# A 31-tap depthwise convolution: 28 taps on TensorE instead of 32, three on VectorE, and two more phases brought over by ScalarE

## Time and profile before

| | us |
|---|---|
| median of 3 runs | 1105.55 (1104.82 to 1106.0) |
| the profiled execution, its time | 1104.8 |
| the profiled execution, its span | 1102.9 |
| TensorE busy | 1089.6, 99% of the span |
| VectorE busy | 668.8, 61% |
| GpSimd busy | 502.6, 46% |
| ScalarE busy | 465.4, 42% |

### The profile page before, as it was taken

The page is one execution under the profiler, slowest core; times in us unless marked ns, Lnnn a source line. Parts: engine busy times, 40 slices in busy tenths (PEclk is TensorE's granted clock), DMA queues, the critical chain, the costliest instruction groups (busy, mean ns, idle before and its releaser), DMA issues.

```text
span 1102.9 us, 16220 instructions
## 1 busy us (share of the span) xinstructions
PE 1089.6 (99%) x5922; PEld 879.0 (80%) x5922; DVE 668.8 (61%) x958; ACT 465.4 (42%) x808; POOL 502.6 (46%) x375
## 2 busy tenths in 40 slices
PE   9999999999999999999999999999999999999997
PEld 7786877788788888888888888877778778888786
DVE  6875986416666666666641222548754757986863
ACT  6436321354744333333333334345464543243663
POOL 5445341122455444444444445433347686632441
PEclk9999999999999999999999999999999999999999
DMA  9953532241223323232323325322115222212222
GB/s 246 136 85 56 67 70 39 84 108 39 78 90 102 114 76 114 76 114 76 114 74 98 105 78 152 115 77 77 39 52 140 54 80 78 77 40 78 77 77 77
DMA packets 101721, 97.28 MB, mean 88 GB/s; under 512 B 4896, under 2 KB 95776, under 8 KB 101280
## 3 DMA queue, kind: packets, MB, share of 16 engines
q1 hardware_dynamic: 101232, 95.71, 31.8%
q10 hardware_dynamic: 432, 0.79, 0.2%
HBM read 94.38 MB, written 2.10 MB: 87 GB/s over the span
## 4 chain that ended last, share of the span: by engine, by line
PE 91%; DVE 4%; ACT 2%; issue 1%; POOL 1%; DMA 1%; POOLq 0%; DVEq 0%; SPq 0%; ACTq 0%
PE ps L1914 26%; PE ps L1916 25%; PE ps L1915 25%; PE ps L2457 4%; PE ps L2118 1%; DVE x_a L1237 1%; DVE conv L1758 1%; PE ps L2392 1%; ACT x_a L674 1%; PE ps L2403 1%; PE ps L2304 1%; PE ps L2286 1%; DVE tt L1349 1%; POOL w_lo L536 1%; PE ps L2380 1%
## 5 line engine op out<-in xcount | busy, mean ns | idle before, releaser
L536 POOL TENSOR_TENSOR w_lo<-raw,w_hi 128x512 fp32r<-128x512 f32 (+1 forms) x330 | 447.9, 1368 | 568.1 <-ACT w_hi L657 557.5
L657 ACT ACTIVATE w_hi<-raw 128x512 fp32r<-128x512 f32 (+1 forms) x330 | 201.1, 620 | 254.1 <-PE ps L1916 237.2
L1914 PE MATMUL ps<-x_a,w_hi 128*128 128x512 f32 x624 | 251.8, 403 | 4.3 <-POOL w_lo L536 2.0
L1916 PE MATMUL ps<-x_a,w_lo 128*128 128x512 f32 x624 | 243.3, 390 | 0.0
L1915 PE MATMUL ps<-x_a,w_hi 128*128 128x512 f32 x624 | 243.3, 390 | 0.0
L1914 PE MATMUL ps<-x_b,w_hi 128*128 128x512 f32 x416 | 162.5, 391 | 0.1
L1915 PE MATMUL ps<-x_b,w_hi 128*128 128x512 f32 x416 | 161.9, 389 | 0.0
L1916 PE MATMUL ps<-x_b,w_lo 128*128 128x512 f32 x416 | 161.8, 389 | 0.0
L1914 PEld LDWEIGHTS ps<-x_a,w_hi 128*128 128x128 f32 x624 | 117.2, 188 | 38.9 <-issue 11.1
L1916 PEld LDWEIGHTS ps<-x_a,w_lo 128*128 128x128 f32 x624 | 117.1, 188 | 24.9
L1915 PEld LDWEIGHTS ps<-x_a,w_hi 128*128 128x128 f32 x624 | 117.3, 188 | 24.6 <-issue 2.2
(11 more groups left out here) (351 smaller groups left out, 1532.2 us busy)
## 6 DMA issues: line engine op xcount, KB each, us to landing
raw<-in_w_up SPq DMA_DIRECT2D x44, 512.0 KB, 4.4
raw<-in_w_in SPq DMA_DIRECT2D x31, 512.0 KB, 7.7
raw<-in_c_w_in SPq DMA_DIRECT2D x24, 512.0 KB, 4.7
raw<-in_a_w_in SPq DMA_DIRECT2D x18, 512.0 KB, 4.6
raw<-in_w_down SPq DMA_DIRECT2D x16, 512.0 KB, 4.4
raw<-in_w_out SPq DMA_DIRECT2D x8, 512.0 KB, 4.0
raw<-in_c_w_out SPq DMA_DIRECT2D x8, 512.0 KB, 4.1
raw<-in_w_down SPq DMA_DIRECT2D x8, 384.0 KB, 3.4
```

The lines of the kernel that those rows point to most:

```text
L536: nc.gpsimd.tensor_tensor(ring_half(WL, n), raw_half(n), f32(ring_half(WH, n)), SUB) \
L657: nc.scalar.activation(ring_half(WH, n), raw_half(n), ACT.Copy).then_inc(w_hi, 1)
L1914: mm(out, w_hi_, x_hi_, start=first, stop=False)
L1916: return mm(out, w_lo_, x_hi_, start=False, stop=last)
```

## The change

The zero tap is gone, and with it a whole step: TensorE does 7 steps of 4 phases, for taps 3 to 30 (`DIRECT` = 3). Taps 0 to 2 are added by VectorE from the unsplit `GLU`, over whole tiles of 128 partitions, in three dependent instructions (`add_direct`). ScalarE, besides phase 3, copies phases 2 and 1 into a new tile `PH`, in eight pieces of 32 partitions (`later_phases`); VectorE adds phase 0 out of PSUM in four pieces, and phases 2 and 1 from `PH` in two instructions over 128 partitions (`add_phases`). ScalarE's and VectorE's work on tile k moves from the end of iteration n = 2k + 4 into iteration n = 2k + 5: on VectorE `add_direct` comes before `evict(n)`, `add_phases` after it and before `glu`; on ScalarE `later_phases` comes after the first weight split. The eviction of the rough mean moves to the start of n = 9, the square of tile 7 on ScalarE to n = 20, of tile 6 to n = 18. The sum of tile 6's square goes behind the last `add_centered`.

```diff
-TAP_STEPS = 8
+TAP_STEPS = 7
+DIRECT = CK - TAP_PHASES * TAP_STEPS
-SQUARES_AT = {11: (0, 1), 13: (2, 3), 15: (4,), 17: (5,), 19: (6, 7)}
+SQUARES_AT = {11: (0, 1), 13: (2, 3), 15: (4,), 17: (5,), 18: (6,)}
+        PH = at("conv_phases", [P, 2, S], F32, AR + 45056)
...
-                                            EYE32[:, :].unsqueeze(1).broadcast_to([P, 32, 32]),
+                                            EYE32[:, :].unsqueeze(1).broadcast_to([P, CK - DIRECT, 32]),
...
-            def last_phase(k):
+            def later_phases(k):
                 act.wait_ge(cv_filled, k + 1)
                 for r in range(4):
                     nc.scalar.activation(CV[32 * r:32 * r + 32, k, :], PS[96:128, 4 + r, :], ACT.Copy) \
                         .then_inc(cv_copied, 1)
+                if k > 0:
+                    act.wait_ge(tile_whole, k)
+                for r in range(4):
+                    for q in (2, 1):
+                        nc.scalar.activation(PH[32 * r:32 * r + 32, q - 1, :], PS[32 * q:32 * q + 32, 4 + r, :],
+                                             ACT.Copy).then_inc(cv_copied, 1)
...
                 if n >= 3:
                     split_hi(2 * u + 3)
+                if n - 1 in CONV_AFTER:
+                    later_phases(CONV_AFTER[n - 1])
...
+                if n == 20:
+                    ln_square(7)
...
-                if n in CONV_AFTER:
-                    last_phase(CONV_AFTER[n])
...
                 if k >= 2:
                     dve.wait_ge(g_hi, k - 1)
                     dve.wait_ge(g_lo, k - 1)
+                    dve.wait_ge(direct_added, k - 1)
...
+            def add_direct(k):
+                dve.wait_ge(cv_copied, 12 * k + 4)
+                for i in range(DIRECT):
+                    by = CK - 1 - i
+                    y = CV[:, k, by:S]
+                    ins = v.scalar_tensor_tensor(out=y, in0=GLU[:, k % 2, 0:S - by], scalar=DCW[:, i, k:k + 1], in1=y,
+                                                 op0=MUL, op1=ADD)
+                    if i < DIRECT - 1:
+                        step(ins)
+                    else:
+                        ins.then_inc(direct_added, 1)
...
             def add_phases(k):
-                for q in (2, 1, 0):
-                    late_by = TAP_PHASES - 1 - q
-                    for r in range(4):
-                        if q == 2:
-                            dve.wait_ge(cv_copied, 4 * k + r + 1)
-                        else:
-                            dve.wait_ge(dchain, steps[0] - 3)
-                        y = CV[32 * r:32 * r + 32, k, late_by:S]
-                        ins = v.tensor_tensor(y, PS[32 * q:32 * q + 32, 4 + r, 0:S - late_by], y, ADD)
...
+                late_by = TAP_PHASES - 1
+                dve.wait_ge(direct_added, k + 1)
+                for r in range(4):
+                    dve.wait_ge(cv_copied, 12 * k + 4 + 2 * r + 2)
+                    y = CV[32 * r:32 * r + 32, k, late_by:S]
+                    v.tensor_tensor(y, PS[0:32, 4 + r, 0:S - late_by], y, ADD).then_inc(cv_ready, 1)
+                dve.wait_ge(cv_ready, 4 * k + 4)
+                for q in (2, 1):
                     late_by = TAP_PHASES - 1 - q
+                    y = CV[:, k, late_by:S]
+                    ins = v.tensor_tensor(y, PH[:, q - 1, 0:S - late_by], y, ADD)
+                    if q == 2:
+                        step(ins)
+                    else:
+                        ins.then_inc(tile_whole, 1)
...
             for n in range(24):
+                if n == SHIFT_AFTER + 1:
+                    dve.wait_ge(shift_filled, 1)
+                    v.tensor_scalar(MEAN, PS[:, (M7 + SHIFT_AFTER + 1) % 4, :], 1.0 / (2 * P), None, MUL) \
+                        .then_inc(bank_free, 1)
+                    dve.wait_ge(bank_free, M7 + SHIFT_AFTER + 2)
+                if n - 1 in CONV_AFTER:
+                    k = CONV_AFTER[n - 1]
+                    add_direct(k)
                 evict(n)
+                if n - 1 in CONV_AFTER:
+                    add_phases(k)
                 if n < 16 and n % 2 == 1:
                     glu(n // 2)
-                if n in CONV_AFTER:
-                    k = CONV_AFTER[n]
-                    add_phases(k)
+                if n - 1 in CONV_AFTER:
...
-                        else:
+                        elif k < KT - 1:
                             add_ln_square(k - 1)
                         add_centered(k)
                         if k == KT - 1:
+                            add_ln_square(k - 1)
                             add_ln_square(k)
...
                 if k >= 1:
-                    pe.wait_ge(cv_ready, k)
+                    pe.wait_ge(cv_ready, 4 * k)
```

More of the change, by code:

```diff
@@ L250, in build @@
         GL = at("glu_lo", [P, 2, GPW], F32R, A3 + 8416)
-        DCWH = at("tap_hi", [P, 32, KT], F32R, A3 + 12736)
-        DCWL = at("tap_lo", [P, 32, KT], F32R, A3 + 13760)
+        DCWH = at("tap_hi", [P, CK - DIRECT, KT], F32R, A3 + 12736)
+        DCWL = at("tap_lo", [P, CK - DIRECT, KT], F32R, A3 + 13760)
         EYE32 = at("eye32", [P, 32], F32, A3 + 14784)
@@ L333, in build @@
         g_hi, g_lo = sem("glu_hi_ready"), sem("glu_lo_ready")
-        cv_filled, cv_copied, cv_ready = sem("conv_filled"), sem("conv_phase_copied"), sem("conv_ready")
+        cv_filled, cv_copied, cv_ready = sem("conv_filled"), sem("conv_phases_copied"), sem("conv_ready")
+        direct_added, tile_whole = sem("direct_taps_added"), sem("conv_tile_whole")
         shift_sum, shift_filled = sem("shift_sum_ready"), sem("shift_filled")
@@ L582, in tap_parts_made @@
                 gp.wait_ge(tap_rounded, 1)
-                nc.gpsimd.tensor_tensor(DCWL[:, 1:32, :], DCW[:, :, :], f32(DCWH[:, 1:32, :]), SUB) \
+                nc.gpsimd.tensor_tensor(DCWL[:, :, :], DCW[:, DIRECT:CK, :], f32(DCWH[:, :, :]), SUB) \
                     .then_inc(tap_parts, 1)
-                gp.wait_ge(tap_parts, 9)
+                gp.wait_ge(tap_parts, 7)
             def tap_weights(k, parts=(0, 1)):
@@ L1070, in _ @@
                 if k == 1:
-                    nc.scalar.activation(DCWH[:, 1:32, :], DCW[:, :, :], ACT.Copy).then_inc(tap_rounded, 1)
+                    nc.scalar.activation(DCWH[:, :, :], DCW[:, DIRECT:CK, :], ACT.Copy).then_inc(tap_rounded, 1)
                 if k >= 1:
@@ L1096, in gated @@
                 act.wait_ge(glu_ready, k + 1)
-                act.wait_ge(tap_parts, 9)
+                act.wait_ge(tap_parts, 7)
                 if k >= 2:
@@ L1740, in glu @@
                 dve.wait_ge(g_hi, k + 1)
-                dve.wait_ge(tap_parts, 9)
+                dve.wait_ge(tap_parts, 7)
                 if k >= 2:
@@ L1765, in center @@
             def center(k):
-                dve.wait_ge(dchain, steps[0])
-                dve.wait_ge(cv_ready, k + 1)
+                dve.wait_ge(tile_whole, k + 1)
                 v.scalar_tensor_tensor(out=CV[:, k, :], in0=CV[:, k, :], scalar=vec("dw_b", k), in1=MEAN,
@@ L1819, in _ @@
             for n in range(24):
+                if n == SHIFT_AFTER + 1:
[6 more added lines that the diff above has]
+                    add_direct(k)
                 evict(n)
+                if n - 1 in CONV_AFTER:
+                    add_phases(k)
                 if n < 16 and n % 2 == 1:
                     glu(n // 2)
-                if n in CONV_AFTER:
-                    k = CONV_AFTER[n]
-                    add_phases(k)
+                if n - 1 in CONV_AFTER:
                     if k == 0:
-                        dve.wait_ge(cv_ready, 1)
+                        dve.wait_ge(tile_whole, 1)
                         step(v.tensor_scalar(ACC[:, :], CV[:, 0, :], vec("dw_b", 0), None, ADD))
                     elif k == 1:
-                        dve.wait_ge(cv_ready, 2)
+                        dve.wait_ge(tile_whole, 2)
                         v.scalar_tensor_tensor(out=ACC[:, :], in0=CV[:, 1, :], scalar=vec("dw_b", 1),
@@ L2468, in ln_sums @@
             def ln_sums():
-                pe.wait_ge(cv_ready, KT)
+                pe.wait_ge(cv_ready, 4 * KT)
                 pe.wait_ge(dsum_ready, 1)
```

16 lines of the change are left out of this document (3 added, 13 removed).

## The result

The changed kernel is slower: median 1107.65 us (1106.06 to 1109.52, 17 runs) against 1105.06 (1104.78 to 1106.0, 17 runs), ratio 1.0023 with a 95% interval of 1.0016 to 1.003, some 2.6 us. That is more than the 2.2 us that the prediction counted as noise. Its executions also lie 3.5 us apart instead of 1.2. The profiled one has a span of 1105.5 us against 1102.9.

The account below looks back on a forecast made before the run. TensorE, busy 1089.6 of 1102.9 us, was taken as the bound. Steps -5.55, VectorE's order +0.6 and channel sums +1.9 gave -3.05 us: 1101.75 for the profiled execution, 1102.5 as median, range 1100.4 to 1105.3.

Parts of the forecast that it names:

- The steps on TensorE: Convolutions on TensorE: one step of 0.694 us fewer in each of 8 tiles, 5.55 us saved, all on the path.
- ScalarE's queue and the weight ring: Eight more ScalarE copies per tile delay weight splits behind them; the ring of four weight halves covers that, cost zero.
- VectorE, in sum: VectorE's round: two us less work, 1.2 to 5 us of GpSimd meetings; 15 to 18.5 us against 16.18 allowed.
- The rough mean: Its sum on VectorE: ready at 13.5 us, 15.9 with two meetings, wanted at 16.1; part of the +0.6 us.
- +0.6 us; the ends are 0 and 2.5: VectorE's order of work up to `cv_ready` and the rough mean, with tile 3's lateness: TensorE waits, +0.6 us altogether.
- The channel sums: TensorE's second channel sum starts later: 1.0 us undisturbed, 2.8 if GpSimd holds up both additions from `PH`; +1.9 taken.
- VectorE eats the gain in the early tiles: Rival: GpSimd meetings make rounds of 17.3 us in tiles 0 to 3; 2.5 back, sums 2.8; 1105.3 us; chance 0.17.
- The slower rival: Rival: `add_direct`'s products meet GpSimd and hold up `cv_ready` in every tile; 1112.4 us at 1.2 us average; chance 0.08.
- The rule on SBUF: VectorE instructions with two SBUF inputs contend with GpSimd reading SBUF, the later fully blocking; taken at its word, 1103.4 us.

Follow-up runs that it names:

- the steps alone: The kernel before with seven tap steps instead of eight, taps 0 to 2 left out, old phases and order: 1099.61 us, ratio 0.9952.
- the rough sum moved forward: The changed kernel with the rough sum that takes in tile 1 right behind add_phases(1), ahead of the glu: 1107.24 us, ratio 1.0019 to the kernel before.
- late splits: The changed kernel with ScalarE's splits of both halves of unit 21 moved behind the square of tile 7: 1105.95 us, ratio 1.0003 to the kernel before.
- no late builds: The changed kernel without GpSimd's building of tap weights for tiles 3 to 7, which reuse those of tiles 1 and 2: 1103.81 us, ratio 0.9986.
- the first filling: The changed kernel with eleven matmuls, 2.5 us, on TensorE ahead of its wait for the rough sum: 1106.38 us, ratio 1.0009 to the kernel before.
- no products: The changed kernel without `add_direct` and the waits on it, taps 0 to 2 left out: 1105.47 us, ratio 1.0003 to the kernel before.
- spread centrings: The changed kernel with the rough mean from tile 0 alone, tiles 0 and 1 centred in the round of n = 8: 1104.62 us, ratio 0.9995.
- the old phases and the products: The kernel of seven steps with old phases, `add_direct(k)` put ahead of the twelve additions out of PSUM: 1151.47 us, ratio 1.0424 to the kernel before.
- both fillings: The changed kernel with eleven matmuls ahead of TensorE's waits for the rough sum and for the channel sums: 1105.3 us, ratio 1.0004.

## Why the prediction was wrong

I had forecast 1102.5 us, 3.05 less than before, with a range up to 1105.3; it became 1107.65, 2.6 more. (The forecast was counted up from a median of three runs, 1105.55; with 17 runs it is 1105.06, and the same sum from there gives 1102.0.)

- *The steps on TensorE*, 5.55 us: right, 5.3 by the ratio of the steps alone.
- *ScalarE's queue and the weight ring*, zero: right for the ring; TensorE waits for no `w_lo` more than before, 0.2 us behind 890 us. But the queue also made ScalarE late for its own copies of tile 1, by 1.1 us, and for that the prediction had no term.
- *"VectorE, in sum"*, two us less and one to five us of meetings: the mechanism was right, the place of the meetings only in part. Products and phase additions together took 3.8 us less over the eight tiles, and the centrings, the glu and the sums of squares, which the term left out, took 10 us more; that is under 1 us more for a round, inside the range of 15 to 18.5. VectorE's rounds held, with no wait at any convolution in the changed kernel. But see the experiment with the rough sum moved forward: at tile 4 VectorE was late too, covered by the delay in front of it.
- *The rough mean*, part of "+0.6 us; the ends are 0 and 2.5": this is the step that failed. It cost 4.4 us by itself. I had the place and the chain, 13.5 us from ScalarE's first copy undisturbed, "with two meetings 15.9, when TensorE wants it 16.1", and took two meetings as the likely case. All five instructions of the chain met GpSimd, which just there had two splits, two builds and two more splits to do, 9.5 us for what I had counted as 4.6. And the chain began 1.1 us late, for ScalarE came to its copies only at 917.94, behind the delayed high part of tile 2 and two splits. I should have read off GpSimd's own timeline, which showed it busy for 14.2 of 17 us in the round before, that hardly an instruction there would pass undisturbed. The prediction even had the reason, but for tile 7 only: ScalarE's splits come right behind its copies, "so GpSimd runs from +8.6". At tile 1 the same happened, from +8.1 us after the first copy (926.03 - 917.94), just as the additions from `PH` began.
- *The clock*: it was in no step and no rival. A wait of 2.7 us cost 4.4. The earlier trace rows showed the full clock all along, and I took it as given also behind the waits that I priced.
- *The channel sums*, "+1.9" between 1.0 and 2.8: the mechanism was right, the size at its upper end. The second sum began 1034.23 - 1019.13 = 15.1 us after ScalarE's first copy, which is the figure I had for both additions held up. I had taken the middle because I thought the order not readable. It was: ScalarE's splits release GpSimd at the very time of the additions.
- *The rivals*: "VectorE eats the gain in the early tiles" came nearest in its two terms, 2.5 and 2.8 us, but it lacked the clock, and its reason, rounds of 17.3 us that pile up, was not what happened. The slower rival, products holding up `cv_ready` in every tile, did not happen either: the products met GpSimd seldom.
- *The rule on SBUF* was borne out in both directions: additions from PSUM stayed at 0.68 us apiece beside a busy GpSimd, those from `PH` took up to 2.13. That one blocks the other fully is nearly so: from 926.03 us two additions and two splits, 1.42 and 2.54 us by themselves, took 3.5 us together, 0.4 less than one after the other.

## What to carry to other kernels

Where one engine is full and another nearly so, price a change by its longest chains up to the points where the full engine waits, each instruction of the chain laid beside what GpSimd does at that time, and not by the round's total. A VectorE instruction over 32 partitions out of PSUM kept its 0.68 us beside a busy GpSimd, where one over 128 partitions with both inputs in SBUF took up to 2.13. Four of the first do what one of the second does, 2.8 us, so the second was still less work here; but its length depends on the moment, and that has to be priced where another engine waits for it. And a wait on TensorE behind which its clock falls costs more than its length: here 1.7 us on top of 2.7, part of which filler matmuls gave back.

## What was not expected of the hardware

The clock. Behind waits of 2.7 to 2.8 us the profiles of this case show it at 0.50, 1.2 GHz, in seven of eight cases (rough mean: the changed kernel and the one with late splits; sums: the rough sum moved forward, no late builds, the first filling, no products, spread centrings; the exception is the changed kernel's sums), and behind the waits of 1.1, 1.6 and 2.2 us there it stayed at 1.00. The length of the wait does not decide it alone. With the old phases and the products, TensorE waited eight times for 3.4 to 6.4 us, and the clock fell every time but one, a wait of 3.46 us. And at the start of the kernel with both fillings it fell after waits of 0.90 and 0.78 us with three matmuls between them, while a single wait of 0.75 us at that place left it at 1.00 in the kernel before. Each of the seven falls cost 1.1 to 1.7 us, counted against the same stretch at full clock. The Trainium skill, TensorE: Matmul & The Clock Gate, Part 1, states that the gated clock knows two levels only, half and full; the rows agree, with 0.50 and 1.00 in all windows that lie on one side. The other: with the same instructions up to there, the first convolution began between 894.4 and 897.2 us, a spread that comes from the first 20 us and from one meeting of VectorE and GpSimd at 140 us; what decides how they fall in an execution is open.
